# Expert kernel: gathered row quarters turned by VectorE, down copies on ScalarE and VectorE, combining shared four, three and one

## The reference

```python
x = x + ga_x * y_x                                   # y_x: the mixers' output @ w_out
h_x = rms_norm(x, norm2_g) * (1 + cf_x) + sf_x       # "modulate"
scores = sigmoid(h_x @ router_w); idx = top_k(scores + router_bias, 8)
wts = scores[idx] / sum(scores[idx]) * 2.5
routed[t] = sum over the 8 experts e of t: wts * (silu(h_x[t] @ w_gate[e]) * (h_x[t] @ w_up[e])) @ w_down[e]
shared = (silu(h_x @ sh_gate) * (h_x @ sh_up)) @ sh_down
out = rms_norm(x + gf_x * (routed + shared), final_norm_g)
```

## Time and profile before

| what | value |
|---|---|
| runs | 2725.13 us median of three (2721.9 to 2731.74) |
| profiled execution | 2728.36 us, its span 2726.7 us |
| PE busy, whole span | 2492.2 us (91%) |
| DVE busy | 1518.7 us (56%) |
| ACT busy | 975.3 us (36%) |
| POOL busy | 842.9 us (31%) |
| DMA, mean | 150 GB/s |

### The profile page before, as it was taken

One profiled execution on the slowest core, in us unless ns is written; L12 is line 12 of the kernel. 1 busy time (PEld: TensorE's weight loads), 2 busy tenths in 40 slices (PEclk: granted clock), 3 DMA queues, 4 the chain that ended last, 5 costly groups with the idle time before them and its releaser, 6 DMA issues. The chain is left out here.

```text
span 2726.7 us, 72339 instructions
## 1 busy us (share of the span) xinstructions
PE 2492.2 (91%) x27195; PEld 1369.5 (50%) x27196; DVE 1518.7 (56%) x2653; ACT 975.3 (36%) x1707; POOL 842.9 (31%) x654
## 2 busy tenths in 40 slices
PE   5999899889799789899879779899999999999977
PEld 2448457735589645699834343333333333333333
DVE  3106355844477712676544476566666666666538
ACT  3613115512222113233211124455555555555411
POOL 1000000000155100111000005566666666666565
PEclk9999998989999999899979889999999999999989
DMA  6001402120000020000032328899988899684177
GB/s 251 15 0 48 143 16 93 49 64 16 1 4 4 3 75 1 2 5 5 6 137 93 128 103 317 333 352 357 358 337 328 331 343 346 252 312 142 70 282 295
DMA packets 109531, 410.21 MB, mean 150 GB/s; under 512 B 21049, under 2 KB 37131, under 8 KB 84236
## 3 DMA queue, kind: packets, MB, share of 16 engines
q1 hardware_dynamic: 77068, 289.81, 29.0%
q0 software_dynamic: 20736, 75.51, 7.4%
q10 hardware_dynamic: 11520, 41.95, 3.9%
HBM read 347.45 MB, written 59.77 MB: 149 GB/s over the span
## 5 line engine op out<-in xcount | busy, mean ns | idle before, releaser
L3282 PE MATMUL bank<-arena 128*32 x1280 | 568.9, 598 | 10.3 <-SPq L68 7.7
L3284 PE MATMUL bank<-arena 128*32 128x512 f32 x3840 | 570.0, 598 | 0.0
L3243 POOL COPY arena<-arena 128x2048 f32 x240 | 449.2, 1906 | 330.8 <-PE bank L3316 317.6
L3282 PEld LDWEIGHTS bank<-arena 128*32 128x32 f32 x1280 | 134.9, 110 | 359.3 <-issue 350.3
L3313 PE MATMUL bank<-arena 128*32 x640 | 289.3, 595 | 5.5 <-POOL arena L3243 5.5
L3316 PE MATMUL bank<-arena 128*32 128x512 f32 x1920 | 290.3, 595 | 0.0
L3437 DVE COPY arena<-arena 128x2048 f32 x80 | 138.7, 1734 | 203.4 <-PE bank L3284 189.3
L3374 ACT COPY arena<-arena 128x2048 f32 x80 | 152.2, 1902 | 168.5 <-PE bank L3284 141.9
L3233 POOL DMA_INDIRECT arena<-normed_rows,arena x80 | 165.0, 2063 | 118.6 <-DVE arena L3421 106.8
L1262 PE MATMUL bank<-arena 64*64 64x64 f32 x4480 | 165.4, 220 | 13.4 <-DVE arena L1334 5.4
L3313 PEld LDWEIGHTS bank<-arena 128*32 128x32 f32 x640 | 70.4, 110 | 197.8 <-issue 197.1
(11 more groups left out here) (553 smaller groups left out, 4625.7 us busy)
## 6 DMA issues: line engine op xcount, KB each, us to landing
arena<-in_exp_w_gate_dram SPq DMA_DIRECT2D x64, 1024.0 KB
arena<-in_exp_w_up_dram SPq DMA_DIRECT2D x64, 1024.0 KB
arena<-in_exp_w_down_dram SPq DMA_DIRECT2D x64, 1024.0 KB
expert_rows<-arena ACTq DMA_DIRECT2D x80, 512.0 KB
arena<-in_w_mod_dram SPq DMA_DIRECT2D x32, 512.0 KB, 7.7
arena<-in_x_dram SPq DMA_DIRECT2D x16, 512.0 KB
arena<-in_w_mod_dram SPq DMA_DIRECT2D x8, 1024.0 KB, 18.3
arena<-in_w_in_dram SPq DMA_DIRECT2D x12, 384.0 KB
```

Of the source, the lines that this page charges most:

```text
L3243: last = nc.gpsimd.tensor_copy(down_copy(u), down_of(slots[u]))
L3282: nc.tensor.matmul(out(SUB - 1), XTT[:, b.q, c, rows(SUB - 1)], W[:, :, c], start=first, stop=end)
L3284: last = nc.tensor.matmul(out(u), XTT[:, b.q, c, rows(u)], WC[:, u, :, c], start=first, stop=end)
```

## The change

- Mixing. The columns of gain and shift are spread to rows by 16 matmuls at the start; VectorE applies both to `XN`; GpSimd copies `XN` into quarters whose columns lie chunk by chunk (`XP`), and SP stores that. The copies of the turned rows are plain.
- Routing. `IDX` gets four entries for each block, one for each quarter of the rows.
- Experts. GpSimd gathers row quarters of 1 KB, four gathers a block, and copies nothing. VectorE turns all of a block's gathered rows with one transpose of 32x32 blocks; TensorE's `turn` and both `flat_half` are gone. Of the three down copies VectorE makes one and ScalarE two. SP issues the down of e-1 after gate and up of e have landed; at the start it issues two gate and up pairs and one down, then waits for the first block's gathers.
- Combining. TensorE adds four rows, VectorE three, ScalarE weights one; the small operations of the norm are done for two tiles together, and at the end the norm of the tile before the last comes ahead of the last tile's sums.

```diff
@@ mixed_out @@
+        @block.gpsimd
+        def _(pool):
+            for t in range(XT):
+                pool.wait_ge(xn, t + 1)
+                if t >= 2:
+                    pool.wait_ge(st[t % 2], 16 * (t // 2))
+                nc.gpsimd.tensor_copy(packed(XP[:, t % 2]), by_quarter(XN[:, t % 2])).then_inc(xp, 1)
...
+            for n, cols in enumerate((k.mul_col[1][0], k.add_col[1][0])):
+                for c in range(KC):
+                    last = nc.tensor.matmul(ps[4 + 2 * n + c // 4][:, (c % 4) * P:(c % 4 + 1) * P],
+                                            cols[:, c:c + 1].to_broadcast([P, P]), k.ident, start=True, stop=True)
+                last.then_inc(spread, 1)
...
+            act.wait_ge(spread, 2)
+            for c in range(KC):
+                last = nc.scalar.copy(ADDS[:, c::KC], ps[6 + c // 4][:, (c % 4) * P:(c % 4 + 1) * P])
+            last.then_inc(add_in, 1)
...
+            dve.wait_ge(spread, 1)
+            for c in range(KC):
+                last = nc.vector.tensor_copy(MULS[:, c::KC], ps[4 + c // 4][:, (c % 4) * P:(c % 4 + 1) * P])
+            last.then_inc(mul_in, 1)
...
-                    nc.vector.tensor_scalar(XN[:, u % 2], X1[:, u], ri[:, u % 2], None, ALU.mult).then_inc(xn, 1)
+                    chain(nc.vector.scalar_tensor_tensor(XN[:, u % 2], X1[:, u], ri[:, u % 2], MULS, ALU.mult, ALU.mult))
+                    nc.vector.tensor_tensor(XN[:, u % 2], XN[:, u % 2], ADDS, ALU.add).then_inc(xn, 1)
@@ shared_and_route @@
-            chain(nc.vector.tensor_copy(IDX[:, 0:NBLK], ps[0][:, 0:NBLK]))
+            quarters = IDX[:, 0:NBLK * SUB].rearrange("p (b q) -> p b q", q=SUB)
+            for q in range(SUB):
+                for r in range(SUB):
+                    last = TS(quarters[r * BR:(r + 1) * BR, :, q], ps[0][q * BR:(q + 1) * BR, 0:NBLK], float(SUB),
+                              float(r), ALU.mult, ALU.add)
+            chain(last)
@@ experts @@
+    row_quarters = xn_dram.rearrange("t (r n) -> (t r) n", r=SUB)
+    def columns(b, u, c):
+        at = ((u + 1) % SUB * KC + c) * BR
+        return XTT[:, b.q, at:at + BR]
...
-            def follow(j, i):
-                e, gates, downs = FROM + j, i * DRING, i * RING
+            def gates(i, e):
                 copied, read = released(at(i, e - RING))
                 hold(sp, hi_d, copied)
                 hold(sp, hi_a, copied)
                 hold(sp, up, read)
                 gate_up(bass.ds(at(i, e), 1), e % RING)
-                hold(sp, down_in[(e - 1) % DRING], downs * 16 + (16 * ((e - 1) // DRING) + 16))
+
+            def gates_landed(i, e):
+                hold(sp, loaded[e % RING], i * (DRING * 32) + 32 * (e // RING + 1))
+                sp.sem_inc(arrived, 1)
+
+            def downs(i, f):
+                if f >= DRING:
+                    copied, read = released(at(i, f - DRING))
+                    hold(sp, dcopy_d, copied)
+                    hold(sp, dcopy_a, copied)
+                    hold(sp, dn, read)
+                down(bass.ds(at(i, f), 1), f % DRING)
+
+            def down_landed(i, f):
+                hold(sp, down_in[f % DRING], i * (RING * 16) + 16 * (f // DRING + 1))
                 sp.sem_inc(down_arrived, 1)
-                copied, read = released(at(i, e - DRING))
-                hold(sp, dcopy, copied)
-                hold(sp, dn, read)
-                down(bass.ds(at(i, e), 1), e % DRING)
-                hold(sp, loaded[e % RING], gates * 32 + (32 * (e // RING) + 32))
-                sp.sem_inc(arrived, 1)
-
-            ROUND, FROM = RING * DRING, DRING
+
+            def follow(i, e):
+                gates(i, e)
+                down_landed(i, e - 2)
+                gates_landed(i, e)
+                downs(i, e - 1)
+
+            ROUND, FROM = RING * DRING, DRING + 1
             sp.sem_inc(st[0], 16)
             sp.sem_inc(st[1], 16)
-            for e in range(RING):
...
+            gate_up(bass.ds(0, 1), 0)
+            down(bass.ds(0, 1), 0)
+            gate_up(bass.ds(1, 1), 1)
+            sp.wait_ge(g_in[0], 16 * SUB)
+            downs(0, 1)
+            gate_up(bass.ds(2, 1), 2)
+            gates_landed(0, 0)
+            down_landed(0, 0)
+            gates_landed(0, 1)
+            gates_landed(0, 2)
+            for e in range(RING, FROM):
+                follow(0, e)
...
-                nc.gpsimd.indirect_dma_start(
-                    out=G[:, b.q], out_offset=None, in_=xn_dram,
-                    in_offset=bass.IndirectOffsetOnAxis(ap=ID[:, b.q], axis=0)).then_inc(g_in[b.q], 16)
-
-            def copy_down(b, n=1):
-                slots = [down_slot_of(pool, b, u) for u in range(SUB - 1)]
-                hold(pool, down_arrived, count_of(pool, b, SUB - 2))
-                if n:
-                    hold(pool, dn, b.n + 1)
-                for u in range(SUB - 1):
-                    last = nc.gpsimd.tensor_copy(down_copy(u), down_of(slots[u]))
-                last.then_inc(dcopy, 1)
+                for q in range(SUB):
+                    nc.gpsimd.indirect_dma_start(
+                        out=G[:, b.q, q], out_offset=None, in_=row_quarters,
+                        in_offset=bass.IndirectOffsetOnAxis(ap=ID[:, b.q, q:q + 1], axis=0)).then_inc(g_in[b.q], 16)
...
+            with pool.Fori(0, NBLK // 2 - 2) as t:
                 for off in range(2):
-                    copy_down(Turn(t, off + 1))
+                    gather(Turn(t, off + 4))
...
         def _(pe):
-            def turn(b, n=1):
-                hold(pe, g_in[b.q], b.half * 16 + 16)
-                if n:
-                    hold(pe, xa, b.n)
-                    hold(pe, xd, b.n)
-                for c in range(KC):
-                    last = nc.tensor.transpose(ps[c // 4][:, (c % 4) * P:(c % 4 + 1) * P], G[:, b.q, c::KC], k.ident)
-                last.then_inc(turned, 1)
...
-            def step(b0, b1, b3):
+            def step(b0, b1):
                 hidden(b1)
                 widen(b0)
                 fold(b1)
-                if b3 is not None:
-                    turn(b3)
...
-            def flat_half(b):
-                hold(act, turned, b.n + 1)
-                for c in range(KC // 2):
-                    last = nc.scalar.activation(XTT[:, b.q, c], ps[0][:, c * P:(c + 1) * P], ACT.Identity,
-                                                bias=k.add_col[1][0][:, c:c + 1], scale=k.mul_col[1][0][:, c:c + 1])
-                last.then_inc(xa, 1)
+            def copy_downs(b, n=1):
+                slots = [down_slot_of(act, b, u) for u in (1, 2)]
+                hold(act, down_arrived, count_of(act, b, 2))
+                if n:
+                    hold(act, dn, b.n + 1)
+                nc.scalar.copy(down_copy(1), down_of(slots[0]))
+                nc.scalar.copy(down_copy(2), down_of(slots[1])).then_inc(dcopy_a, 1)
...
                     high(b2, slot)
                 store(b0)
                 fold(b1)
-                if b3 is not None:
-                    flat_half(b3)
+                copy_downs(b1)
...
-            def flat_half(b):
-                hold(dve, turned, b.n + 1)
-                for c in range(KC // 2, KC):
-                    last = nc.vector.tensor_scalar(XTT[:, b.q, c], ps[1][:, (c - 4) * P:(c - 3) * P],
-                                                   k.mul_col[1][0][:, c:c + 1], k.add_col[1][0][:, c:c + 1],
-                                                   ALU.mult, ALU.add)
-                last.then_inc(xd, 1)
+            def turn(b, n=1):
+                hold(dve, g_in[b.q], b.half * 64 + 64)
+                if n:
+                    hold(dve, up, b.n)
+                nc.vector.transpose(XTT[:, b.q], G[:, b.q].rearrange("p q n -> p (q n)")).then_inc(turned, 1)
+
+            def copy_down(b, n=1):
+                slot = down_slot_of(dve, b, 0)
+                hold(dve, down_arrived, count_of(dve, b, 0))
+                if n:
+                    hold(dve, dn, b.n + 1)
+                nc.vector.tensor_copy(down_copy(0), down_of(slot)).then_inc(dcopy_d, 1)
...
                     high(b2, slots)
                 store(b0)
                 if b3 is not None:
-                    flat_half(b3)
+                    turn(b3)
                 if b5 is not None:
                     index(b5)
+                copy_down(b1)
@@ combine @@
-    BY_DVE = 3
+    BY_DVE = 4
...
-                if t >= 2 and s < BY_DVE:
-                    pool.wait_ge(used, (t - 2) * BY_DVE + s + 1)
+                if t >= 2 and s == 0:
+                    pool.wait_ge(first, t - 1)
+                if t >= 2 and 0 < s < BY_DVE:
+                    pool.wait_ge(used, (t - 2) * (BY_DVE - 1) + s)
                 if t >= 2 and s == BY_DVE:
                     pool.wait_ge(summed, t - 1)
...
+            def first_row(t):
+                n = t * TOPK
+                act.wait_ge(g_in[n % NB], 16 * (n // NB + 1))
+                if t >= 2:
+                    act.wait_ge(mix, t - 1)
```

(58 more changed lines are left out.)

129 lines of the change are left out of this document (49 added, 80 removed).

## The result

The changed kernel takes 2832.76 us (median of 4, 2826.36 to 2833.79) beside 2725.52 us for the kernel before (median of 4): ratio 1.0375, 95% interval 1.0355 to 1.0395. It is slower, as forecast, but by 107 us and not by 35, and outside the range.

The account below looks back on a forecast made before the run. TensorE was taken to set the experts' pace, with the DMA engines nearly full beside it. The terms +21 + 8 + 3 + 3 + 2.5 + 2 + 1.6 - 6 = +35 on 2725 gave 2760 us, range 2695 to 2805 (8 in 10).

Parts of the forecast that it names:

- the weights' queue: Experts: downs requested only after gates land, 12.8 us an expert in dense stretches, partly given back; +8 us (0 to +40).
- mixing: Mixing stage: broadcast matmuls and copies at the start +3 us, longer VectorE and GpSimd work at the end +3 us.
- routing: Routing: one copy becomes 16 small operations of 0.15 us each, with a little between them; +2.5 us.
- the combining: Combining stage: TensorE loses one row of five, partly offset by the DMA engines; together -6 us (-14 to 0).
- the ring: Experts' step: dependency chain from ScalarE's down copies through VectorE and back, 12.03 us against 11.77 now; +21 us.
- `fold` to the copy: Experts, ScalarE: from `fold` to the next first down copy, three register reads, wait and copy start; 2.1 us.
- Rival B: Experts: the weights' queue is the bound, some 50 experts take 13.2 us; +58 instead of +8, 2810 us; chance 0.17.
- Rival A: Experts: the ring is shorter than read, step falls to 11.1 to 11.3 us; about 2690 us, faster; chance 0.18.
- Packets: Experts' gathers: 530 to 576 packets a step from 1 KB rows load the DMA engines, +0.7 us a step.
- first block: Experts' start: the weights' queue waits for four gathers before it tells of landed gates; +2 us (-3 to +5).
- last block: Experts' end: GpSimd's copies become store, `fold` and two copies on ScalarE; +1.6 us.
- The turn on VectorE: Experts: one 128x1024 transpose on VectorE replaces four 128x128 operations there; 1.25 us, hidden.

Follow-up runs that it names:

- the first experiment: Changed kernel with the down weights of e-1 requested right behind the gates of e, before these land: 2762.24 us, ratio 1.0116 to the kernel before.

## Why the prediction was wrong

- **The failed step is the weights' queue, +8 us.** I saw that the downs would be asked for behind a landing, and gave it 12.8 us an expert where an expert fills one block, with a range of 12.4 to 13.9. The rate measured is 13.53, so the idle queue alone costs 1.6 us an expert (13.53 - 11.77 - 0.14), and I had put 0 to 1.5 on it. But what failed is the credit: "three slots and the experts with two blocks give it back", bounded by +40. They don't. From its first request for gates to its last the queue took 896.3 us, where it took 806.5: +89.8, beside +88.9 for the 77 steps. From the last request to the last `low` copy it is 147.5 us, and was 146.3. Had each of the 63 intervals been 1.76 us late, it would be 111 us, so about a fifth was given back (estimate). My reading: the mean over the stage would allow the rate (79 x 12.34 / 64 = 15.2 us an expert), but with three slots the queue can't run far ahead, so a dense stretch pays its lateness, and a late block frees its slot late as well: after the wait at 1915.72 the next gates went out 21.5 us behind the last. No run has more slots. With the order undone the stage loses 67 us, and on the old kernel the late order costs 75, 69 in its steps.
- **Without that one line the forecast stands.** With the order undone the ratio is 1.0116, +32 us on that chip, where I had +35 (+27 without the queue's term). Some of that is luck: mixing and routing came out 7.2 and 6.2 us longer there (forecast 6 and 2.5), the combining 3.0 us shorter and not 6, and the experts' stage 28 us longer and not 33. The free steps are 12.10 us there, 77 x 0.33 = +25 for the +21 of the ring. In the changed kernel itself they are 12.35, +45: every term of the ring holds but `fold` to the copy, 2.51 for 2.1, and this gap is the shorter one (1.65 + 0.37 = 2.0) in most steps once the queue is mended. The longer gap goes with the long table load (the first experiment has the counts); why that load comes more often beside the late queue is not shown.
- **Rival B** named the right mechanism, with a chance of 0.17 and 13.2 us an expert: 2810, and its sign came too (`low` copies that wait for landed weights). Its miss of 23 us is 10 in the steps (88.9 for its 21 + 58), 9 in the other stages and the rest of this one, and what the profile and the median differ by.
- **Rival A** had its mechanism in no step: the ring was not shorter than read. Its prize was real: with reads and order mended the step is 10.9 us.
- **Packets**: +0.7 us a step was too much by 0.6. The step that failed is the count: the gathers' 1 KB rows travel in packets of 4 KB, 188 packets a step and not 530 to 576. This error went the other way and was inside the 12.8.
- **Routing**: +2.5, measured +6.0. The 16 small operations take 4.91 us, 0.31 each and not 0.15; they read a bank and write whole numbers, 32x80. The row that I took was of 128x1.
- **Mixing, first block, last block, combining**: +6, +2, +1.6, -6 against +4.5, +2.2, +3.7, -4.7. These errors are small and partly cancel. The combining did meet the DMA engines: share 1.01 at 400 GB/s, TensorE busy 71.84 of 80.
- **The turn on VectorE**, 1.25 us by the estimate, takes 1.23 and is hidden.
- **The limit of about 358 GB/s** (the Trainium skill, "DMA: Bandwidth & Descriptors", Where 436 GB/s comes from): over the stretch of the earlier trace rows the experts of no run pass 362 GB/s, but the combining holds 400 over 80 us. The measurement decides, and as in the prediction the page was not the bound.

## What to carry to other kernels

When a change moves a transfer request behind a wait for another landing, price it as lost rate for each transfer, and give no credit for slack elsewhere unless the slots can hold it. Two bounds that idle together (TensorE 0.77, DMA 0.80) pointed here to a late request, with the DMA engines at a share of 0.12 and 0.03 around two landings. And register reads belong ahead of the last wait, beside a running operation: 1.7 to 2.2 us of every step were three table reads behind a wait.

## What was not expected of the hardware

- A table read into a register takes 280 ns to load; with its operations about 0.6 us. In three of four steps of the changed kernel one of ScalarE's three loads takes over 600 ns (793 in the step shown). It stands beside VectorE's `index` and down copy (2615.06, 2615.10) and GpSimd's first gather (2615.94). Over the stage, a gather starts within 55 of the 66 long loads and within 7 of the 167 others, so the gathers are the likeliest; it was not tried, and stays open.
- Queued behind a 1.9 us copy, the same reads cost nothing, on ScalarE and on GpSimd.
- Rows of 1 KB, gathered four at a time, show as packets of 4 KB and cost the DMA engines 0.05 to 0.14 us a block more than whole rows, at nearly the same bytes.
- A VectorE copy of 128x2048 took 3.72 us beside GpSimd's copies, 1.22 alone.
- After gaps TensorE came back at the lower of its two clocks: 45.0 us of its busy time with the late downs alone, 5.3 before.
- The DMA engines moved 400 GB/s over 80 us of combining, 377 before.
